# The second FFN's in-projection as seven block products in place of eight, with FFN tiles in groups of 6, 6, 6 and 4

## What is computed

```python
def rms_norm(x, eps=EPS):
    xf = x.astype(jnp.float32)
    return (xf * lax.rsqrt(jnp.mean(xf * xf, axis=-1, keepdims=True) + eps)).astype(x.dtype)

def modulate(x, shift, scale):
    return rms_norm(x) * (1.0 + scale) + shift

def swiglu(h, w_in, w_out):
    g, u = jnp.split(h @ w_in, 2, axis=-1)
    return (jax.nn.silu(g) * u) @ w_out
...
        xc = xc + mc[5] * swiglu(modulate(xc, mc[3], mc[4]), w_ffn_in[i], w_ffn_out[i])
        xs = xs + ms[5] * swiglu(modulate(xs, ms[3], ms[4]), w_ffn_in[i], w_ffn_out[i])
    y_prompt = rms_norm(xc) * g_final
    y_sample = rms_norm(xs) * g_final
```

## Time and profile before

| | us |
|---|---|
| median of 3 runs | 1735.05 |
| the runs, lowest and highest | 1734.57, 1735.76 |
| span of the profiled execution | 1734.7 |
| PE busy in it | 1681.0 |
| DVE busy in it | 976.8 |
| ACT busy in it | 572.7 |
| PE's first matmul of the second FFN starts at | 1252.73 |
| the last unit of its in-projection ends at | 1679.9 |

### The profile page before, as it was taken

One profiled execution on the slowest core, in us unless ns is written; L12 is line 12 of the kernel. 1 busy time (PEld: TensorE's weight loads), 2 busy tenths in 40 slices (PEclk: granted clock), 3 DMA queues, 4 the chain that ended last, 5 costly groups with the idle time before them and its releaser, 6 DMA issues.

```text
span 1734.7 us, 27685 instructions
## 1 busy us (share of the span) xinstructions
PE 1681.0 (97%) x11355; PEld 1573.5 (91%) x11355; DVE 976.8 (56%) x1783; ACT 572.7 (33%) x928; POOL 78.3 (5%) x58
## 2 busy tenths in 40 slices
PE   6899996999999999999999999999999999999998
PEld 3589984689999999999999996688999999999998
DVE  4624489566687658765866366744644334433445
ACT  4432563553421112212225444343432112211223
POOL 0000074000000000000000202000000000000000
PEclk8899997999999999999999999999999999999999
DMA  9346223203443444335315203001322232214212
GB/s 314 118 137 216 72 94 99 80 2 97 116 147 106 126 139 146 110 103 153 107 45 183 73 26 100 25 1 49 110 73 61 58 104 81 62 49 122 58 46 80
DMA packets 236567, 168.55 MB, mean 97 GB/s; under 512 B 7669, under 2 KB 232139, under 8 KB 236076
## 3 DMA queue, kind: packets, MB, share of 16 engines
q1 hardware_dynamic: 235540, 166.32, 31.8%
q10 hardware_dynamic: 920, 0.69, 0.2%
HBM read 161.13 MB, written 5.87 MB: 96 GB/s over the span
## 4 chain that ended last, share of the span: by engine, by line
PE 92%; DVE 2%; SPq 2%; POOL 1%; DMA 1%; ACT 1%; issue 0%; ACTq 0%; DVEq 0%
PE ua L1005 13%; PE ub L1005 13%; PE ua L1007 13%; PE ua L1006 12%; PE ub L1007 12%; PE ub L1006 12%; PE ua L1237 2%; PE ub L1237 1%; PE pm L1264 1%; PE pt L1264 1%; SPq L599 1%; PE pt L1342 1%; PE ua L1248 1%; DVE sct L2259 1%; PE pm L921 0%
## 5 line engine op out<-in xcount | busy, mean ns | idle before, releaser
L1856 ACT ACTIVATE whi<-raw 128x2048 fp32r<-128x2048 f32 (+2 forms) x101 | 144.1, 1427 | 628.3 <-PE ua L1007 311.9
L2116 DVE TENSOR_TENSOR wlo<-raw,whi 128x2048 fp32r<-128x2048 f32 (+2 forms) x118 | 208.6, 1767 | 93.4 <-ACT whi L1628 63.4
L1005 PE MATMUL ub<-in_a_high,whi 128*128 128x384 f32 (+1 forms) x720 | 225.6, 313 | 0.0
L1007 PE MATMUL ub<-in_a_high,wlo 128*128 128x384 f32 (+1 forms) x720 | 224.0, 311 | 0.0
L1006 PE MATMUL ub<-in_a_rest,whi 128*128 128x384 f32 (+1 forms) x720 | 223.5, 310 | 0.0
L1005 PE MATMUL ua<-in_a_high,whi 128*128 128x384 f32 (+1 forms) x704 | 220.0, 313 | 0.0
L1007 PE MATMUL ua<-in_a_high,wlo 128*128 128x384 f32 (+1 forms) x704 | 219.0, 311 | 0.0
L1006 PE MATMUL ua<-in_a_rest,whi 128*128 128x384 f32 (+1 forms) x704 | 218.6, 310 | 0.0
L1005 PE MATMUL ua<-in_b_high,whi 128*128 128x256 f32 (+2 forms) x696 | 217.8, 313 | 0.0
L1007 PE MATMUL ua<-in_b_high,wlo 128*128 128x256 f32 (+2 forms) x696 | 216.4, 311 | 0.0
L1006 PE MATMUL ua<-in_b_rest,whi 128*128 128x256 f32 (+2 forms) x696 | 215.7, 310 | 0.0
(11 more groups left out here) (614 smaller groups left out, 2868.3 us busy)
## 6 DMA issues: line engine op xcount, KB each, us to landing
raw<-in_w_ffn_in SPq DMA_DIRECT2D x88, 512.0 KB, 4.8
modw<-in_w_mod SPq DMA_DIRECT2D x38, 1024.0 KB, 5.3
raw<-in_w_ffn_out SPq DMA_DIRECT2D x32, 512.0 KB, 3.9
raw<-in_w_in_even SPq DMA_DIRECT2D x10, 1024.0 KB, 7.8
raw<-in_w_in_odd SPq DMA_DIRECT2D x7, 1024.0 KB, 5.4
raw<-in_w_ffn_out SPq DMA_DIRECT2D x16, 384.0 KB, 3.4
mod_first<-in_w_mod SPq DMA_DIRECT2D x5, 1024.0 KB, 11.8
mod_tail<-in_w_mod SPq DMA_DIRECT2D x4, 1024.0 KB, 6.4
```

What stands on the lines that cost most here:

```text
L1005: pe.matmul(dst, wh, xh, start=first, stop=False)
L1007: return pe.matmul(dst, wl, xh, start=False, stop=last)
L1856: act.activation(whi[s][:, 0:width] if dst is None else dst, raw[s][:, 0:width], ACT.Copy).then_inc(w_hi, 1)
L2116: dve.tensor_tensor(lo, src[s][:, 0:width], hi.bitcast(F32), ALU.subtract).then_inc(w_lo, 1)
```

## The change

The in-projection of the second FFN uses the Winograd form of Strassen's scheme on 2 x 2 blocks. For one FFN tile the weights are four blocks: gate and up, each over the first four k-tiles (A11, A21) and the last four (A12, A22). The input has four blocks: first and second four k-tiles by the first and second 320 tokens (X11, X12, X21, X22). The seven products are each 4 k-tiles of three matmuls over 322 columns (320 and the two shift columns), 84 matmuls:

- P1 = A11 X11, P2 = A12 X21, P5 = (A21 + A22)(X12 - X11), P6 = (A21 + A22 - A11)(X22 - X12 + X11), P3 = (A12 - A21 - A22 + A11) X22, P7 = (A11 - A21)(X22 - X12), P4 = A22 (X22 - X12 + X11 - X21).
- Gate: P1 + P2 and P1 + P6 + P5 + P3. Up: P1 + P6 + P7 - P4 and P1 + P6 + P7 + P5.

PE adds P6 and then P7 onto P1 in its bank, and P3 onto P5. Values that are needed before something is added to them are copied out by ScalarE first (`snapped`); VectorE makes the four sums for the outputs (`combined`), and four sums of weight blocks of 512 columns (`weight_sum`), which are split into high and rest as the plain weights are. The blocks of the input and their sums are built once, in the out-projection ahead (`x_tile`). Raw weights now have four buffers of 1024 columns ("quarters"). The lists are written out without loops, the groups are 6, 6, 6 and 4, the first FFN is unchanged, and the load of the final gain, which stood ahead of the FFN, comes at its end since the buffer is in use till then. Some semaphores are shared by several users; this moves nothing.

```diff
 GROUPS = (8, 8, 6)
+GROUPS_1 = (6, 6, 6, 4)
+LH = T // 2
+HW = LH + 2
...
-            sp.dma_start(gain[:, :], i_["g_final"].rearrange("(a d) -> a d", a=1).to_broadcast([P, D])).then_inc(fin_g, 16)
+
+            def quarter_load(q, src, kt):
+
+                if q in (2, 3):
+                    sp.wait_ge(w_lo, U_FFN1)
+                elif q >= 4:
+                    sp.wait_ge(g_lo, quarter_user(q - 4))
+                sp.dma_start(quarter(q, 0, kt * P).rearrange("p (k n) -> p k n", k=kt), src).then_inc(q_ld[q % 4], 16)
...
+            sp.wait_ge(unit_done, out_p[-1])
+            sp.dma_start(gain[:, :], i_["g_final"].rearrange("(a d) -> a d", a=1).to_broadcast([P, D])).then_inc(s_vec, 16)
...
+            def product(f, name, k0=0, k1=4):
+
+                bank, group, block, src = {
+                    "P1": (0, 0, 0, lambda k: (xa_hi[:, k, 0], xa_lo[:, k, 0])),
+                    "P2": (1, 0, 1, lambda k: (xb_hi[k][:, :], xb_lo[k][:, :])),
+                    "P5": (2, 1, 0, lambda k: (xa_hi[:, k, 1], xa_lo[:, k, 1])),
+                    "P6": (0, 1, 1, lambda k: (xq_hi[k][:, 1], xq_lo[k][:, 1])),
+                    "P3": (2, 2, 1, lambda k: (xq_hi[k][:, 0], xq_lo[k][:, 0])),
+                    "P7": (0, 2, 0, lambda k: (xq_hi[k][:, 2], xq_lo[k][:, 2])),
+                    "P4": (1, 3, 0, lambda k: (xq_hi[k][:, 3], xq_lo[k][:, 3]))}[name]
+                dst = fast_set(in_u[f])[:, bank, 0:HW]
+                wh, wl = (ring(t, in_g[f] + group, 1024)[:, block * 512:(block + 1) * 512] for t in (whi, wlo))
...
+                    pe.matmul(dst, wh[:, c], xh, start=first, stop=False, skip_group_check=True)
+                    pe.matmul(dst, wh[:, c], xl, start=False, stop=False, skip_group_check=True)
+                    ins = pe.matmul(dst, wl[:, c], xh, start=False, stop=last, skip_group_check=True)
+                if k1 == 4:
+                    ins.then_inc(unit_done, 1)
...
+            def fast_in_unit(f):
+                g = in_g[f]
+                pe.wait_ge(g_lo, g + 1)
+                bank_free(in_u[f])
+                product(f, "P1")
+                if f == 0:
+                    pe.wait_ge(g_lo, g + 2)
+                    product(f, "P5")
+                    product(f, "P2", 0, 3)
+                    pe.wait_ge(sn_ok, 1)
+                    product(f, "P6", 0, 3)
+                    product(f, "P2", 3, 4)
+                    product(f, "P6", 3, 4)
+                    norm_sum(3)
+                else:
+                    product(f, "P2")
+                    pe.wait_ge(g_lo, g + 2)
+                    product(f, "P5")
+                    pe.wait_ge(sn_ok, 4 * f + 1)
+                    product(f, "P6")
+                pe.wait_ge(g_lo, g + 3)
+                pe.wait_ge(sn_ok, 4 * f + 2)
+                product(f, "P3")
+                pe.wait_ge(sn_ok, 4 * f + 3)
+                product(f, "P7")
+                pe.wait_ge(g_lo, g + 4)
+                pe.wait_ge(f_add, 4 * f + 1)
+                product(f, "P4")
...
+            def fast_out_units(e):
+                kt = GROUPS_1[e]
+                for m in range(2):
+                    fast_out_begin(e, m)
+                    fast_out_part(e, m, 0, kt - 1)
+                for m in range(2):
+                    fast_out_part(e, m, kt - 1, kt).then_inc(unit_done, 1)
+                for m in range(2, KD):
+                    fast_out_begin(e, m)
+                    fast_out_part(e, m, 0, kt).then_inc(unit_done, 1)
...
+            def snapped(f, n):
+
+                bank, name, scale = ((0, "P1", 1.0), (2, "P5", 1.0), (0, "P6", 1.0), (1, "P4", -1.0))[n]
+                act.wait_ge(unit_done, after_product(f, name))
+                if n == 0 and f:
+                    act.wait_ge(f_add, 4 * f - 2)
+                elif n == 1 and f:
+                    act.wait_ge(f_add, 4 * f)
+                elif n == 2:
+                    act.wait_ge(f_add, 4 * f + 1)
+                elif n == 3:
+                    act.wait_ge(f_add, 4 * f + 3)
+                act.activation(snap[n % 2][:, :], fast_set(in_u[f])[:, bank, 0:HW], ACT.Copy, scale=scale).then_inc(sn_ok, 1)
...
+            def fast_in(e, f):
+                first, last = f == FIRST_F[e], f == FIRST_F[e] + GROUPS_1[e] - 1
+                if not first:
+                    snapped(f - 1, 3)
+                if f:
+                    in_high(f, 2)
+                snapped(f, 0)
+                in_high(f, 3)
+                if f == 0:
+                    snapped(f, 1)
+                    norm_scale(3)
+                if not first:
+                    hidden_high(f - 1)
+                if last:
+                    out_high_(e, 0)
+                else:
+                    in_high(f + 1, 0)
+                if f:
+                    snapped(f, 1)
+                snapped(f, 2)
+                if last:
+                    out_high_(e, 1)
+                else:
+                    in_high(f + 1, 1)
+                gate_silu(f)
...
+            def combined(f, n):
+
+                bank, name, half = ((1, "P2", 0), (2, "P3", 1), (0, "P7", 1), (0, "P4", 0))[n]
+                dve.wait_ge(unit_done, after_product(f, name))
+                dve.wait_ge(sn_ok, 4 * f + (1, 3, 2, 4)[n])
+                if n == 0 and f:
+                    dve.wait_ge(hid_f, NF + f)
+                if n == 2:
+                    dve.wait_ge(g_pre, NF + f + 1)
+                dve.tensor_tensor(sums[:, half, :], fast_set(in_u[f])[:, bank, 0:HW], snap[(0, 0, 1, 1)[n]][:, :], ALU.add
+                                  ).then_inc(f_add, 1)
+
+            def scaled(f, n, dst):
+                dve.wait_ge(f_add, 4 * f + 2 * n + 2)
+                return dve.tensor_tensor(halves(dst[:, :]), sums[:, :, 2:HW], halves(rstd[:, 0, :]), ALU.mult)
...
+            def fast_in(e, f):
+                first, last = f == FIRST_F[e], f == FIRST_F[e] + GROUPS_1[e] - 1
+                if not first:
+                    up_second(f - 1)
+                if f:
+                    in_rest(f, 2)
+                if not first:
+                    hidden_product(f - 1)
+                if not last:
+                    weight_sum(f + 1, 0)
+                gate_first(f)
+                in_rest(f, 3)
+                if not last:
+                    weight_sum(f + 1, 1)
+                if not first:
+                    hidden_rest(e, f - 1)
+                if last:
+                    out_rest(e, 0)
+                else:
+                    in_rest(f + 1, 0)
+                gate_second(f)
+                if last:
+                    out_rest(e, 1)
+                else:
+                    in_rest(f + 1, 1)
+                combined(f, 2)
+                if not last:
+                    weight_sum(f + 1, 2)
+                    weight_sum(f + 1, 3)
...
+            def hidden_last(e):
+                f = FIRST_F[e] + GROUPS_1[e] - 1
+                up_second(f)
+                out_rest(e, 2)
+                hidden_product(f)
+                if e < len(GROUPS_1) - 1:
+                    out_rest(e, 3)
+                hidden_rest(e, f)
+                if e == len(GROUPS_1) - 1:
+                    out_rest(e, 3)
+
...
+                if m == 1:
+                    dve.wait_ge(s_vec, 80)
+                if m >= 1:
+                    result_gain(m - 1)
```

650 lines of the change are left out of this document (482 added, 168 removed).

## The result

The changed kernel took **1711.14 us** (median of 4 runs, 1708.40 to 1712.92) against 1735.40 for the kernel before beside it; the ratio is **0.9843, 95% interval 0.9821 to 0.9866**, that is 1.6% faster. The forecast was 1706.5, with a range of 1700 to 1721. The profiled execution has a span of 1708.1 us, where the kernel before had 1734.7.

The account below looks back on a forecast made before the run. PE was taken as the bound, through the number and length of its matmuls. -38.3 us for fewer matmuls, +9.1 for new waits and +0.6 for late VectorE waits gave -28.6, so 1706.5 us, range 1700 to 1721.

Parts of the forecast that it names:

- The matmuls: In-projection on PE: 84 matmuls a unit at 0.148 us in place of 96, -38.3 us over 22 units.
- VectorE hidden: In-projection units: VectorE busy 11.5 us of 12.47, staying just under PE and so hidden.
- waits met late: VectorE in the in-projection units: an added price of 0 to 0.7 us, taken as 0.6.
- cushion of 3.6 us: In-projection units: weights, P3 and P4 ready some 3.6 us early, so VectorE may fall behind that much before PE notices.
- P6 and P7 of the first unit: PE waits for ScalarE's copies of P1 and of P1 + P6: +1.0 and +2.9 us.
- Tile 2 of three out-projections: Groups 1 to 3: tile 2 needs tile 0's bank, showing 0.55 us each, +1.7 us in all.
- Last group's hidden rest: Out-projection of the last group: 5.2 us chain behind 18 matmuls of 3.15 us, +2.1 us less the earlier 0.25.
- First transpose, gain: End of the kernel: first transpose waits 0.4 us more for its residual; late gain costs +1.2 us at the third.
- Nothing lost in front of the FFN: Ahead of the second FFN: no time lost was expected there.
- The clock: PE's clock after P7's wait in the first unit: the forecast, chance 0.60, included no loss from a drop.
- rival 1: First unit: clock drops at P7's wait, half clock for some 10 us loses 5 us, giving 1711; chance 0.13.
- the median is 0.35 above that execution: Final step from the profiled execution to the median: 1706.1 us becomes 1706.5 us.

Follow-up runs that it names:

- f2: Changed kernel with P1 of every unit computed twice, so a unit has 96 matmuls of 322 columns again: 1746.33 us.
- f1: Kernel before with only the second FFN's groups changed to 6, 6, 6 and 4, eight products kept: 1742.32 us, ratio 1.0037.
- f3: Changed kernel with ScalarE's P1 + P6 copy and weight copy ahead of the first unit's roots, and four more orders changed: 1704.95 us, ratio 0.9823.
- g3: f3 with groups of 6, 6, 5 and 5 and one k-tile more ahead of the first out-projection tile's last: 1701.02 us, ratio 0.9781.
- the control: Changed kernel run once more with no edit: 1711.61 us, ratio to before 0.9854.
- g4: Changed kernel with ScalarE's P1 + P6 copy and weight copy ahead of the roots, plus seven PE pauses ahead of P3: stage 468.6 us, one run.

## Why the prediction was right, point by point

- **The matmuls.** -38.3 forecast from 0.148 us a matmul; the trace has 0.1475 to 0.148, a unit of 12.44 for 12.47 (0.7 us less in 22 units), f2 gets 0.147 from the other side, and the distance over all traces is some 39 us. Right, and the reason for the result.
  The Trainium skill's distance (TensorE: Matmul & The Clock Gate, "Wait — 56ns, not 53.3ns?", N / 2.4 GHz + 2.5 ns) is an estimate of 0.137 us for 322 columns. The trace differs, with 0.0105 us more for each matmul than that, so the measured distance decides.
- **VectorE hidden.** Right, with 10.7 us busy where 11.5 were summed; the 0.6 for waits met late did not appear. The conclusion held, its ground did not: the **cushion of 3.6 us** was the wrong step. It followed VectorE's copy, sum, scaling and weight rest to P3 and left out what ScalarE has in front of its copy of P5. Measured it is 0.9 us. Two more sums in a unit, which the prediction's working would have called free, cost 6.4.
- **P6 and P7 of the first unit.** 1.0 and 2.9 forecast; brackets 0.84 and 2.57, with 0.25 each 1.1 and 2.8. Right, by the chain named.
- **Tile 2 of three out-projections.** 0.55 forecast, 0.50 in brackets, 0.75 in time. Right in place, 0.2 short each.
- **Last group's hidden rest.** 2.1 forecast, 2.02 and 0.25. Right. This and tile 2 are what the groups were priced at, 2.1 and 1.7; with the 0.25 of each wait they measure 2.3 and 2.2. The 4.8 us of f1 don't check these terms one by one: in the order of before other waits open (three for a hidden rest, two in the last group).
- **First transpose, gain.** 0.4 and 0.40. The gain came late as forecast, and VectorE idled 2.64 us for it, but PE's third transpose shows 0.38 and not 1.2. VectorE's timeline there:

```profile
1675.13 0.56 DVE L2799 TENSOR_TENSOR yout<-pm,gain 128x384 f32<-128x384 f32 x1 [2.64 <-DMA gain<-in_g_final]
```

- **Nothing lost in front of the FFN.** Wrong. The queue and PE's timeline in the changed kernel:

```profile
1199.93 0.99 SPq L869 DMA_DIRECT2D raw<-in_w_ffn_in  x2
1201.28 9.43 SPq L757 DMA_DIRECT2D raw<-in_w_out_odd  x3
```

```profile
1210.29 0.44 PE L1109 MATMUL ub<-in_b_high,whi 128*128 128x384 f32 x1 [1.28 <-DVE wlo L2438]
```

  The change issues the FFN's first two weight loads ahead of the out-projection's third, which the prediction should have counted among what is moved; the wait before that tile is 1.28 where it was 0.54. f3 and g3 put the load back in front, and there it is gone.
- **The clock.** The likeliest case had it at full; it fell, in the trace of the change and in the control. This is rival 1, put at 0.13 with 1711 us. Its ground (a wait of 2.9 beside one of 2.88 that brought the fall) was the better evidence, and the chance was too small. Its price was too large, 5 us for the 2.8 and 1.5 measured. That the median meets its 1711 is luck: the smaller loss came together with the next point.
- **From span to time.** The step "the median is 0.35 above that execution" set a time beside a span. In every run (1.8 in g4) time is 2.2 to 2.4 us above span, with and without the change, so the forecast span of 1706.1 meant about 1708.4 for such an execution.

Together, for the profiled execution: 1706.1 forecast, +2.8 for the clock, +0.3 for the later start of the FFN, +0.6 for tile 2, -0.6 for waits met late, -0.7 for the units, -0.6 for the gain, and +0.2 of small ones make the 1708.1 measured; the 2.3 us from span to time on top, where 0.4 were taken, and the spread of the runs (1706.2 to 1710.7) make the median of 1711.1. So the sign and the size rest on what the prediction said, and the 4.6 us that it missed are the clock and a step of bookkeeping.
